# First branch's first pair of products: which token block arrives already split

## The reference

```
h      = rms_norm(x, norm_w);   proj = h @ w_in + b_in
u_a    = attention(...) * silu(a_z)            # first mixer's output, 1024 x 1024
u_m    = sigmoid(m_o) * head_norm(mlstm(...)) * silu(m_z)     # second mixer's output
merged = sigmoid(g_attn) * (u_a @ w_branch_attn) + sigmoid(g_mlstm) * (u_m @ w_branch_mlstm)
out    = rms_norm(x + merged @ w_out, final_norm_w)
```

## Time and profile before

| what | value |
|---|---|
| time, median of 3 runs | 1067.73 us (1067.67 to 1067.8) |
| the profiled execution's own time | 1067.98 us |
| its span, first to last instruction | 1066.2 us |
| granted TensorE clock, mean over the span | 0.998 of full speed |
| PE busy | 1052.9 us, 99% of the span |
| DVE, ACT, POOL busy | 777.2, 539.3, 683.3 us |

### The profile page before, as it was taken

The page is one execution under the profiler, slowest core; times in us unless marked ns, Lnnn a source line. Parts: engine busy times, 40 slices in busy tenths (PEclk is TensorE's granted clock), DMA queues, the critical chain, the costliest instruction groups (busy, mean ns, idle before and its releaser), DMA issues.

```text
span 1066.2 us, 18684 instructions
## 1 busy us (share of the span) xinstructions
PE 1052.9 (99%) x6343; PEld 854.3 (80%) x6343; DVE 777.2 (73%) x1188; ACT 539.3 (51%) x1286; POOL 683.3 (64%) x467
## 2 busy tenths in 40 slices
PE   8999999999999999999999999999999999999997
PEld 6887787887877888888888887888878788888886
DVE  5964785775866867776867695778779747766897
ACT  7544754745746643454445454644468345113543
POOL 3567555556555469658975697569858994545441
PEclk9999999999999999999999999999999999999999
DMA  7235133132152142233323323232329549766324
GB/s 222 66 93 96 41 108 90 42 120 69 39 154 64 52 146 81 56 85 120 101 87 90 120 88 108 89 118 87 89 83 350 168 144 326 254 243 256 164 99 138
DMA packets 122078, 131.79 MB, mean 124 GB/s; under 512 B 7884, under 2 KB 97288, under 8 KB 120472
## 3 DMA queue, kind: packets, MB, share of 16 engines
q1 hardware_dynamic: 107048, 84.42, 26.2%
q10 hardware_dynamic: 14960, 46.47, 12.9%
HBM read 96.16 MB, written 34.70 MB: 123 GB/s over the span
## 4 chain that ended last, share of the span: by engine, by line
PE 95%; DVE 2%; ACT 1%; DVEq 0%; DMA 0%; issue 0%; ACTq 0%
PE ps L1169 69%; PE ps L1510 8%; PE ps L1076 4%; PE ps L1281 3%; PE ps L1262 2%; PE ps L1336 2%; PE ps L1408 1%; PE ps L1390 1%; PE ps L1405 1%; ACT ev L1600 1%; DVE s_lo L2809 1%; PE ps L1402 1%; PE ps L1356 1%; PE ps L1423 1%; PE ps L1395 1%; PE ps L1118 1%
## 5 line engine op out<-in xcount | busy, mean ns | idle before, releaser
L844 POOL TENSOR_TENSOR ring_lo<-w,ring_hi 128x512 fp32r<-128x512 f32 x142 | 207.0, 1479 | 85.8 <-ACT ring_hi L1642 85.7
L844 POOL TENSOR_TENSOR ring_lo<-t,ring_hi 128x512 fp32r<-128x512 f32 x108 | 157.0, 1459 | 142.0 <-ACT ring_hi L1642 142.0
L1169 PE MATMUL ps<-s_hi,ring_hi 128*128 128x512 f32 x560 | 222.3, 397 | 0.0
L1169 PE MATMUL ps<-s_lo,ring_hi 128*128 128x512 f32 x560 | 218.9, 391 | 0.0
L1169 PE MATMUL ps<-s_hi,ring_lo 128*128 128x512 f32 x560 | 218.8, 391 | 0.0
L1169 PE MATMUL ps<-h_hi,ring_hi 128*128 128x512 f32 x420 | 165.8, 395 | 0.0
L1169 PE MATMUL ps<-h_lo,ring_hi 128*128 128x512 f32 x420 | 164.3, 391 | 0.0
L1169 PE MATMUL ps<-h_hi,ring_lo 128*128 128x512 f32 x420 | 163.9, 390 | 0.0
L1642 ACT ACTIVATE ring_hi<-w 128x512 fp32r<-128x512 f32 x144 | 86.6, 623 | 107.3 <-PE ps L1169 90.3
L1169 PEld LDWEIGHTS ps<-s_hi,ring_hi 128*128 128x128 f32 x560 | 105.2, 188 | 22.8 <-issue 2.5
L1169 PEld LDWEIGHTS ps<-s_hi,ring_lo 128*128 128x128 f32 x560 | 105.2, 188 | 21.9
(11 more groups left out here) (330 smaller groups left out, 2088.6 us busy)
## 6 DMA issues: line engine op xcount, KB each, us to landing
w<-in_w_in SPq DMA_DIRECT2D x128, 256.0 KB, 3.1
xs<-in_x SPq DMA_DIRECT2D x8, 512.0 KB, 7.5
ga_scratch<-ev ACTq DMA_DIRECT2D x4, 1024.0 KB, 4.1
u_scratch<-silu_z ACTq DMA_DIRECT2D x8, 512.0 KB, 3.2
c_rows<-c_scratch ACTq DMA_DIRECT2D x8, 512.0 KB, 6.6
ev<-u_scratch SPq DMA_DIRECT2D x8, 512.0 KB, 4.9
u_sums_scratch<-ev ACTq DMA_DIRECT2D x4, 1024.0 KB, 5.0
gm_scratch<-ev ACTq DMA_DIRECT2D x4, 1024.0 KB, 5.1
```

The lines of the kernel that those rows point to most:

```text
L844: return nc.gpsimd.tensor_tensor(flat(lo[:]), flat(raw_or_sum[:]), flat(hi[:]).bitcast(F32), ALU.subtract)
L1169: mm = nc.tensor.matmul(ps[:, bank, columns], w[:, k, :], h[:, k, columns], start=(m == 0), stop=(m == PRODUCT - 1))
```

## The change

Which of the seven blocks comes split from the second mixer is set by a constant, `SPLIT = 3`, where it was block 6.

- The second mixer's steps split the sum in `ev[:, 0, token_half(1)]` (block 3's) instead of the one in `ev[:, 1, token_half(0)]` (block 6's). Kinds, sizes and number of these instructions stay.
- SP loads block 3 as two transfers, high and low, and block 6 as one. The places of the blocks in SP's order stay.
- ACT's `block_high(3)`, which stood between `after(5)` and `after(6)` of pair 31, goes; `block_high(6)` is added in pair 32 at q = 2, ahead of `store_gm` and `head_roots`.
- DVE's `block_low(3)`, the last of the second mixer's last step, goes; `block_low(6)` is added in pair 32 at q = 2, behind `c11`.
- PE waits for the two transfers before product 7 (block 3), and for ACT and DVE at product 3 (block 6). `block_count` gives the new counter values. The matmuls stay the same, in the same order.

```diff
+SPLIT = 3
+def block_count(n):
+    return n + 1 if n < SPLIT else n
...
-                if n == 6:
-                    sp.dma_start(s4[0][:].bitcast(F32), scr_uh.rearrange("k p n -> p k n")).then_inc(u_in[n], 16)
-                    into = s4[1][:].bitcast(F32)
+                if n == SPLIT:
+                    sp.dma_start(s3[0][:].bitcast(F32), scr_uh.rearrange("k p n -> p k n")).then_inc(u_in[n], 16)
+                    into = s3[1][:].bitcast(F32)
...
-                    if n < 6:
-                        pe.wait_ge(u_hi, n + 1)
+                    if n != SPLIT:
+                        pe.wait_ge(u_hi, block_count(n))
                     else:
                         pe.wait_ge(u_in[n], 32)
...
-                        for n in {1: (0,), 4: (1,), 5: (2, 3), 6: (4,)}.get(q, ()):
+                        for n in {1: (0,), 4: (1,), 5: (2,), 6: (4,)}.get(q, ()):
                             block_high(n)
...
-                        A(us_hi[:], ev[:, 1, token_half(0)], ACT.Copy).then_inc(s_hi, 1)
+                        A(us_hi[:], ev[:, 0, token_half(1)], ACT.Copy).then_inc(s_hi, 1)
...
                     if a == 0 and q == 2:
+                        block_high(6)
                         store_gm(PAIRS - 1)
...
                             weights_low(ring3, w12, w7_hi, w7_ready)
-                            block_low(3)
...
             def block_low(n):
-                dve.wait_ge(u_hi, n + 1)
+                dve.wait_ge(u_hi, block_count(n))
...
-                        if q < 2:
+                        if q < 3:
                             block_low(4 + q)
```

More of the change, by code:

```diff
@@ L1446, in in_parts @@
                     part(product_bank(n, None), ring_slot[1], hi)
-                    if n < 6:
-                        pe.wait_ge(u_split, n + 1)
+                    if n != SPLIT:
+                        pe.wait_ge(u_split, block_count(n))
                     return part(product_bank(n, None), ring_slot[0], lo, last=True)
@@ L2116, in _ @@
                         for k in range(KT):
-                            act.wait_ge(u_in[k // 2], 32)
+                            act.wait_ge(u_in[k // 2], 48 if k // 2 == SPLIT else 32)
                             A(um_part(k)[0], um_full(k), ACT.Copy).then_inc(u_hi, 1)
@@ L2704, in branch_sum_low @@
                     dve.sem_inc(passed, 1)
-                    part = ev[:, 1, token_half(0)]
+                    part = ev[:, 0, token_half(1)]
                     V.tensor_tensor(part.bitcast(F32R), part, us_hi[:].bitcast(F32), ALU.subtract).then_inc(us_made, 1)
```

## The result

| | before | changed |
|---|---|---|
| median of 22 runs each | 1067.87 us (1066.93 to 1068.62) | 1069.09 us (1068.40 to 1071.49) |
| span of the profiled execution | 1066.2 us | 1067.0 us |

The ratio is 1.0014, with a 95% interval of 1.0008 to 1.002: 1.2 us slower, less than 0.2%, and clear of no change.

A forecast was written before the change was run, and what follows sets the result against it. PE, busy 99%, bounds the kernel, with 2.09 us of gaps behind alternating DVE and POOL low parts. PE's 0.9 us gain in pair 32 can't be kept; POOL 1.2 us later gives 1068.9 us, range 1067.5 to 1070.2.

The forecast's parts named there:

- The size of the prize: PE in pair 32: three gaps, 2.09 us or 0.196% of the time, are all there is to win.
- The transfers: DMA: block 3's extra MB, 2.7 us, delays those behind it; blocks 4, 5, 6 land at 821.6, 825.3, 828.0.
- The ladder: DVE's and POOL's low parts exclude each other and alternate; first_sum of pair 33 ends at 835.35, 1.2 us later.
- the start of split 5: DVE's block_low(5), behind POOL's low_4 (ends 827.0), can't start before 827.3 and ends at 829.5.
- split 6: DVE's block_low(6), asked for near 830 and so ahead of POOL's low_3, ends at 832.8.
- PE in pair 32: No wait at product 7; gaps of 0.45 and 0.35 us at products 5 and 3; end 0.9 us earlier.
- Where the gain goes: Behind pair 32: POOL 1.2 us later makes turn_h and product 4 of pair 33 1.2 us later.
- The sum: Whole kernel: +1.2 us, 1068.9 us against the median of 1067.73.
- the slower rival: Block 4 lands 2 us later still, at 823.6; 1070.6 us; decides from a landing near 822.9; chance 0.15.
- PE keeping its gain: PE keeps the 2.09 us; needs first_sum ahead of block_low(6) or engines that don't exclude each other; 1065.7 us; chance 0.07.
- the gaps only move: Block 4 lands before 821.1, pair 32 gains and POOL takes it back at turn_h; 1067.7 us; chance 0.16.

The follow-up runs named there:

- e1: Changed kernel with block 3's low half requested behind block 5 instead of right behind its high half: 1067.66 us against 1067.61 for the kernel before.
- e5: Changed kernel with DVE filling block 6's low part with zeros instead of subtracting (output not the reference's): 1067.18 us against 1067.75 for the kernel before.
- e6: Kernel before with low_1 and low_2 of pair 33 made by DVE instead of POOL: 1067.69 us against 1067.75 unedited.
- e2: Changed kernel with POOL making low_3 of pair 32 ahead of low_4 and low_5: 1067.83 us against 1067.61 for the kernel before.
- e3: Changed kernel with block 4 requested behind block 5: 1071.72 us against 1067.61 for the kernel before.
- e9: e1 with low_1, low_2 and low_6 of pair 33 made by DVE instead of POOL: 1067.97 us against 1067.75 for the kernel before.
- e4: Changed kernel with a second copy on ACT replacing DVE's low part of block 6 (output not the reference's): 1069.11 us against 1067.61 for the kernel before.

## Why the prediction was right, step by step

**The size of the prize.** 2.09 us of gaps in pair 32. e1 closed all three, and pair 32 took 19.04 us, as worked out from the spacing of the groups.

**The transfers.** Blocks 4 and 5 were said to land where the next MB landed before: 821.6 and 825.3, block 6 at 828.0. Less the 0.25 us between the traces that is 821.35, 825.05 and 827.75; measured 821.4, 824.1 and 827.0. Block 4's place was right to 0.1 us. Blocks 5 and 6 were put 0.9 and 0.7 us too late: the extra microsecond that block 6's pair had in the trace of before did not come with the place in the queue (more on it in the last section).

**The ladder.** `first_sum` of pair 33 was to end at 835.35, 1.2 us later. It ended at 834.93, or 1.0 us later from the start of pair 32. The term that was mis-sized is the start of split 5: it could follow `low_4` at once, since block 5 was there earlier. Each further step took what was forecast, to 0.1 us: 3.3 us from the end of split 5 to that of split 6, 1.14 for `low_3`, a pause of 0.22 and 1.29 for `first_sum`. That the removed split doesn't shorten it, because three splits stand ahead of `first_sum` either way, was right, and e5, with two, shows what the third is worth: 1.8 us of the median, 1.5 at product 4.

**PE in pair 32.** Forecast: no gap at product 7, small ones at the second groups of products 5 and 3 behind POOL, and an end 0.9 us earlier. All seen (0.46 us of the weight loads' time and 0.28 of PE's own). The end came 1.2 us earlier: without the wait behind it the pair takes 834.51 + 0.91 - 815.47 = 19.95 us, where it took 21.13.

**Where the gain goes.** Right in substance: POOL takes it back. The place was put too late. The text named `turn_h` and product 4 of pair 33; PE met POOL already at product 1 (0.83 us), then at product 6 (0.26), and only 0.17 us were left at `turn_h`, since `low_1` was as late as all that stands behind it. `turn_h` itself came 0.83 us later, product 4 0.96: before, PE took up `turn_h` 0.19 us after `normalised_h` had ended, and at product 4 it was already waiting.

**The sum.** +1.2 us was forecast. The two profiles show +0.96 and +1.19 at product 4, the medians +1.2. The mechanism is the one that was forecast; that the sum fits to the tenth is in part luck. In the first profile `first_sum` is 1.0 us late and not 1.2, and a second profile differs by 0.23 us at product 4. And the landing of block 4 was read off one execution: with the 9.6 us that block 5 took in e6 in place of 8.4, the same working gives 813.19 + 9.6 = 822.8, just short of the 822.9 from which the slower rival was to begin.

The Trainium skill's page "SBUF — State Buffer", section "Who interferes with whom", says that a DVE instruction with at most one SBUF input, outside the modes that use both ports, does not contend with GpSimd. The trace of e5 agrees: the fill took 1.76 us and `low_3` beside it 1.30, where `first_sum` without such company took 1.29.

**The rivals.** PE keeping its gain did not happen, nor in e1, where its premise (`first_sum` ahead of split 6) was tried and failed by 0.9 us. That the gaps only move is what e1 and e2 are: with block 4 early, or with `low_3` out of the way, the time is that of before. The slower case is e3: block 4 at 824.1, 2.7 us later, costs 2.9 us more by the medians and 2.55 by the profiles, so the price of 1 us for each us was right. From which landing on block 4 begins to cost was not tested: the changed kernel and its variants take it up either early (e1, 818.64) or at 821.4 and later.

## What to carry to other kernels

Moving a step off the engine that ends the waits of one stage wins nothing if a second engine, which shares a resource with it, has the same number of such steps ahead of what the next stage waits for. Write the two engines' operations in one list, with the order in which they ask, and count up to the first operation that the next stage needs. And a block that arrives already split is two transfers instead of one, 2 MB for 1. Here, where the DMA engines were full, the second MB put off blocks 4 and 5, which stand behind it, by some 2.7 us. Ask for the part that is needed last behind the blocks that others wait for, as e1 does.

## What was not expected of the hardware

The two halves of block 6 took 9.4 and 11.7 us to land in the trace of before; those of block 3 in the changed kernel, through the same queue, 8.5 and 10.8, and the three single blocks behind them 11.2, 11.2 and 11.3. The extra microsecond is not the pair's: it comes and goes from one execution to the next. In e6, with the transfers of before, block 6's high half landed 2.7 us behind block 5 and not 3.7, but block 5 itself had landed 1.2 us later. And e1 and e9 have the same transfers, and block 3's low half, behind block 5 in both, took 11.6 us in e1 and 10.8 in e9. What it is stays open.

And a 256 KB load that took 2.7 us in the trace of before took 5.3 us in e4, 0.3 us behind the request of a 1 MB store from another queue, and 3.0 us in e5, 2.5 us behind it.
